# Expert products with a narrower gather ring, one resident half of the query weights, and weighted sums on four 64x64 quadrants

## The chip, the cores and the metric

The kernel runs on one core of a Trainium2 chip. The metric is the device time of one execution in microseconds. Three executions of the kernel before took 1419.11 us in the median (1418.01 to 1419.7); the execution that was profiled took 1418.62 us, of which the span from its first to its last instruction is 1416.6 us.

## The reference

Two transformer blocks follow each other on 256 tokens of width 1024, all in float32. The change lies in the second block, at its end. There the attention's result is added to `x`, and then each token is sent through experts:

```python
h2 = rms_norm(x, g_ffn) * (1.0 + scale2) + shift2
x = x + gate2 * peer_ffn(h2, w_peer_q, peer_keys1, peer_keys2, peer_u, peer_v)
return rms_norm(x, g_final)
```

```python
q = (hc @ w_q).reshape(-1, PEER_HEADS, PEER_KEY_DIM)         # 8 heads
...                                                          # top 16 of 128 x 128 keys for each head
g = softmax(best_s)
act = gelu(einsum('cd,chkd->chk', hc, u[expert]))            # one dot product for each expert
out = einsum('chk,chkd->cd', g * act, v[expert])             # weighted sum of rows of v
```

Each token has 8 x 16 = 128 experts of its own, and each expert is a row of 1024 numbers of `u` and one of `v`.

## The kernel before

The 256 tokens are two tiles of 128, one token on each partition. A *set* `n` (0 to 255) is one expert for each token of a tile: sets 0 to 127 belong to tile 0, 128 to 255 to tile 1. For each set five engines do one step, in this order:

- GpSimd (POOL, L2594) issues an indirect DMA, the *gather*: for each of 128 tokens one row of `peer_uv` (u and v side by side, 8 KB), 1 MiB in all, into a *ring slot*.
- VectorE (L2392) multiplies the u half with the tokens and sums: the *product*.
- ScalarE (L1544) takes the gelu of it.
- GpSimd (L2566) lays a 128x128 *diagonal* matrix with the weight of each token.
- TensorE (L1116) multiplies this diagonal with the v half, 1024 columns in two halves, and adds into two PSUM banks: the *sum*. With the sum the ring slot is free again.

The order on each engine is written out by hand. Each engine has a function `until(tick)` that does its step for all sets up to a tick, and between such calls stands the rest of tile 1's work (projections, attention, output rows, queries). TensorE's sums stand two ticks behind (`LAG`). GpSimd runs a loop over the gathers: before gather `n` into a slot that held set `b`, it lays the diagonals up to `b + LEAD` (`LEAD` is 2) and then waits for the sum of `b`. So with `m` slots gather `n` needs the diagonal of set `n - m + 2` and the sum of set `n - m`. The function `slot_table` deals the slots out in turn; `JOIN` says at which set further slots join.

Before, seven slots are there at first: `first_slot`, a tile of its own, and six halves of the weight ring `wr` (three tiles of 2 MiB), which are free when `w_out` and the query weights `w_peer_q` have been used for tile 0. `xc` joins at set 7, three places of the arena at set 88 and two more at set 118; so there are 8 slots to set 87, 11 to set 117, 13 then.

Tile 1's weights for the second block come once more from memory, in 18 *pieces* of 0.86 or 1 MiB which SyncE loads (L551, L560) into three buffers of the arena, later two, in turn; each waits for the piece that its buffer held. Pieces 0 and 1 are loaded before the ring starts, 2 to 4 just before, the rest beside the gathers. Pieces 14 to 17 are the query weights, used by `peer_queries` (L1087). The logits of the queries against the keys are `key_scores` (L1098), and the products of tile 1's output rows with `w_out` stand at L1277.

When all sums of a tile are there, VectorE multiplies them with the gate and adds them to `x` (L2490 and L2492 for tile 1, in two halves of 512 columns; the first half waits for `half_done`, the second for `pe_used`).

Of the kernel before, what the change touches and what calls it, by code (L numbers as in the profile page):

```python
# [26 lines left out]
SLOTS, DIAGS, LAG, LEAD = 7, 8, 2, 2  # L27
# [155 lines left out]
JOIN = {SLOTS: 1, 88: 3, 118: 2}  # L183
# [114 lines left out]
def program(nc, A, out):  # L298
    ctx = ExitStack()
    with ctx:  # L300
# [100 lines left out]
        piece = [region(kb0, KT * 256) for kb0 in (50, 58, 66)]  # L401
# [40 lines left out]
        p_in = [sem(f"p_in{i}") for i in range(3)]  # L442
# [44 lines left out]
        def _(sp):  # L487
# [18 lines left out]
            for i, (name, src, k, cols, _, _) in enumerate(blocks):  # L506
# [32 lines left out]
                if name == "tok":  # L539

                    sp.wait_ge(s["wuk_zero"], 1)
                    sp.dma_start(wuk[:, :, ROPE:], A["w_uk_2"][0]).then_inc(s["small_in"], 16)
# [4 lines left out]
                    for n, key in enumerate(("peer_keys1_2", "peer_keys2_2")):
                        sp.dma_start(keys[:, n * 64:(n + 1) * 64], A[key][0]).then_inc(s["ffg_in"], 16)
                    sp.wait_ge(s["ada_used"], 12)
                    for j in range(2):  # L550
                        sp.dma_start(piece_land(j), pieces[j]).then_inc(p_in[j], 16)  # L551
# [4 lines left out]
            for j in range(2, len(pieces)):  # L556
# [1131 lines left out]
        def _(dve):  # L1688
# [677 lines left out]
            def until(tick):  # L2366

                while dotted[0] < min(tick, SETS):
# [116 lines left out]
            dve.wait_ge(s["half_done"], 1)  # L2485
            for n in range(2):
                c = slice(n * BANK, (n + 1) * BANK)
                if n:
                    dve.wait_ge(s["pe_used"], SETS)
                chain(V.tensor_tensor(gated[:, n, :], bank[n][:, :], modb[:, 3, c], ALU.mult))  # L2490
                chain.wait()
                V.tensor_tensor(x[:, 1, c], x[:, 1, c], gated[:, n, :], ALU.add).then_inc(s["x_final"], 1)  # L2492
# [10 lines left out]
        def _(pool):  # L2503
# [66 lines left out]
            for n in range(SETS):  # L2570
# [5 lines left out]
                if n == 1:  # L2576
                    pool.wait_ge(s["wout_ready"], 2)
                elif n == 3:
                    pool.wait_ge(s["pair_ready"], filled("pq01"))
                elif n == 5:  # L2580
                    pool.wait_ge(s["pair_ready"], filled("pq03"))
                elif n == SLOTS:
                    pool.wait_ge(s["h2_done"], 1)
                elif n in JOIN:
                    if JOIN[n] == 3:
                        pool.wait_ge(s["pv_ready"], 2 * UNITS)
                        pool.wait_ge(s["oss_done"], 4)
                    else:
                        pool.wait_ge(s["pair_ready"], filled("ks13b"))
# [31 lines left out]
```

## Time and profile before

| | us |
|---|---|
| median of three executions | 1419.11 |
| profiled execution | 1418.62 |
| its span | 1416.6 |
| TensorE busy | 1297.8 (92%) |
| VectorE busy | 833.9 (59%) |
| GpSimd busy | 428.2 (30%) |
| gathers (software queue), share of the 16 DMA engines' span | 47.5%, 275.99 MB |
| SyncE's transfers (hardware queue) | 30.2%, 154.50 MB |

Times in the trace count from the first instruction. The gathers begin at 725.65 us and the last product is done at about 1406 us, so the expert stage is nearly half of the execution. A busy share is an average over the whole span; the stage has its own limits, which the rows below show. TensorE's busy time there contains the time in which a matmul's result is still on its way, so two matmuls overlap in it.

### The profile page before, as it was taken

The numbers are of one execution on the slowest core, as the hardware profiler recorded it, in microseconds if no ns is written. First come the engines' busy times: TensorE is split into PE (matmuls) and PEld (weight loads), VectorE is DVE, ScalarE is ACT, GpSimd is POOL, SyncE is SP. The second block draws the span as 40 slices with busy tenths as digits, with TensorE's granted clock in tenths as the row PEclk, the third lists the DMA queues.
The fourth block names the chain that finished last, engine by engine and source line by source line (L and its number), as shares of the span: only waits on it lengthen the run. The fifth ranks groups of instructions, "written<-read, shape, count | busy, mean of one in ns | idle before, by whom it ended". The sixth has DMA issues, their size and how long they took to land.

```text
span 1416.6 us, 15143 instructions
## 1 busy us (share of the span) xinstructions
PE 1297.8 (92%) x5447; PEld 837.6 (59%) x5447; DVE 833.9 (59%) x2027; ACT 275.0 (19%) x670; POOL 428.2 (30%) x554
## 2 busy tenths in 40 slices
PE   7999999999999999999989999989997777777776
PEld 6888888888687777757666644445642222222222
DVE  3553466213138888733486678757666767766654
ACT  2013100130010000033333234432220112111101
POOL 0101030000100000000024455555566555655551
PEclk9999999999999999999999999999999999999999
DMA  8345665224468888577369999999999999999995
GB/s 290 121 159 190 230 139 179 79 101 149 134 238 316 291 314 290 185 263 280 120 273 423 422 424 420 422 411 410 425 425 425 425 426 424 426 425 426 425 427 229
DMA packets 120202, 431.46 MB, mean 305 GB/s; under 512 B 10950, under 2 KB 34956, under 8 KB 84544
## 3 DMA queue, kind: packets, MB, share of 16 engines
q0 software_dynamic: 37904, 275.99, 47.5%
q1 hardware_dynamic: 82224, 154.50, 30.2%
q8 instruction: 44, 0.72, 0.2%
q14 instruction: 30, 0.25, 0.0%
HBM read 429.23 MB, written 1.24 MB: 304 GB/s over the span
## 4 chain that ended last, share of the span: by engine, by line
PE 59%; DMA 29%; DVE 3%; issue 3%; POOL 3%; ACT 2%; SPq 0%; POOLq 0%; DVEq 0%; ACTq 0%
PE psum L588 31%; DMA wr<-peer_uv,arena 13%; DMA arena<-peer_uv,arena 9%; PE psum L1116 6%; PE psum L890 4%; DMA first_slot<-peer_uv,arena 4%; DMA xc<-peer_uv,arena 3%; PE psum L968 2%; PE psum L866 2%; PE psum L941 2%; PE psum L1134 1%; POOL arena L2566 1%; PE psum L639 1%; POOL wr L2594 1%; PE psum L1178 1%
## 5 line engine op out<-in xcount | busy, mean ns | idle before, releaser
L588 PE MATMUL psum<-hT,wr 128*128 128x256 f32 x1792 | 391.6, 380 | 1.8 <-DMA wr<-in_w_in 1.8
L588 PEld LDWEIGHTS psum<-hT,wr 128*128 128x128 f32 x1792 | 339.1, 190 | 51.7 <-issue 6.0
L1116 PE MATMUL psum<-wr,arena 128*128 128x512 f32 x576 | 276.0, 609 | 39.1 <-POOL arena L2566 38.9
L2392 DVE CUSTOM_DVE_ANT_0 wr<-psum,wr 128x1024 f32<-128x1024 f32 x144 | 176.1, 1223 | 108.8 <-DMA wr<-peer_uv,arena 108.6
L1116 PEld LDWEIGHTS psum<-wr,arena 128*128 128x128 f32 x576 | 102.6, 193 | 178.9 <-issue 177.7
L2566 POOL TENSOR_SCALAR arena<-cst,arena 128x128 f32<-128x128 f32 x256 | 121.4, 474 | 171.5 <-ACT arena L1544 163.3
L2594 POOL DMA_INDIRECT wr<-peer_uv,arena x144 | 144.0, 1000 | 84.5 <-PE psum L1116 60.7
L1116 PE MATMUL psum<-arena 128*128 128x512 f32 x256 | 125.9, 616 | 33.6 <-POOL arena L2566 33.6
L1544 ACT ACTIVATE arena<-arena 128x1 f32<-128x1 f32 x256 | 50.9, 202 | 488.1 <-DVE arena L2392 487.8
L2392 DVE CUSTOM_DVE_ANT_0 arena<-psum,arena 128x1024 f32<-128x1024 f32 x64 | 78.4, 1224 | 55.5 <-DMA arena<-peer_uv,arena 55.5
L1116 PEld LDWEIGHTS psum<-arena 128*128 128x128 f32 x256 | 44.2, 191 | 111.4 <-issue 111.3
L2549 POOL TENSOR_TENSOR arena<-arena 128x512 f32<-128x512 f32 x11 | 16.9, 1538 | 217.6 <-DVE arena L1719 217.6
L2008 DVE SCALAR_TENSOR_TENSOR arena<-arena,csil 128x512 f32<-128x512 f32 x96 | 79.2, 825 | 3.0
L1717 DVE TENSOR_SCALAR arena<-psum,vec 128x256 f32<-128x256 f32 x68 | 29.8, 479 | 86.4 <-PE psum L588 78.5
L1719 DVE SCALAR_TENSOR_TENSOR arena<-psum,vec,arena 128x255 f32<-128x255 f32 (+1 forms) x160 | 69.7, 477 | 2.8
L2594 POOL DMA_INDIRECT arena<-peer_uv,arena x64 | 64.4, 1006 | 19.8 <-issue 11.3
L2594 POOL DMA_INDIRECT first_slot<-peer_uv,arena x24 | 24.0, 998 | 123.1 <-DVE arena L2340 108.4
L1116 PE MATMUL psum<-first_slot,arena 128*128 128x512 f32 x96 | 47.9, 622 | 8.6 <-POOL arena L2566 8.6
L588 PE MATMUL psum<-arena,wr 128*128 128x256 f32 x256 | 55.7, 379 | 0.0
L890 PE MATMUL psum<-wr,arena 128*128 128x512 f32 x128 | 55.6, 592 | 0.0
L1116 PE MATMUL psum<-xc,arena 128*128 128x512 f32 x96 | 46.3, 604 | 7.3 <-POOL arena L2566 7.1
L588 PEld LDWEIGHTS psum<-arena,wr 128*128 128x128 f32 x256 | 48.5, 190 | 7.3 <-issue 0.8
(350 smaller groups left out, 1422.6 us busy)
## 6 DMA issues: line engine op xcount, KB each, us to landing
wr<-in_w_in SPq DMA_DIRECT2D x22, 2048.0 KB, 8.8
arena<-in_w_ada SPq DMA_DIRECT2D x12, 2048.0 KB, 9.9
wr<-in_w_up SPq DMA_DIRECT2D x22, 1024.0 KB, 8.3
arena<-piece SPq DMA_DIRECT2D x16, 1024.0 KB, 9.1
wr<-in_w_down SPq DMA_DIRECT2D x5, 2048.0 KB, 9.7
wr<-in_w_a_out SPq DMA_DIRECT2D x2, 2048.0 KB, 8.1
wr<-in_w_b_out SPq DMA_DIRECT2D x2, 2048.0 KB, 8.6
wr<-in_w_o SPq DMA_DIRECT2D x2, 2048.0 KB, 8.1
```

What stands on the lines that cost most here:

```text
L588: mm = nc.tensor.matmul(bank[p % 4][:, f * S:(f + 1) * S], slot(i)[:, k, n * P:(n + 1) * P], act[:, k, :], start=k == 0, stop=k == KT - 1)
L866: mm = nc.tensor.matmul(bank[4 + 2 * n + t][:, :], sgb[:, k, t * P:(t + 1) * P], slot(23 + n)[:, k, :], start=k == 0, stop=k == KT - 1)
L890: mm = nc.tensor.matmul(bank[4 + 2 * n + t][:, :], act_ffn[:, f, t * P:(t + 1) * P], slot(i)[:, row, n * BANK:(n + 1) * BANK], start=f == ...
L941: mm = nc.tensor.matmul(o[:, 0:2 * cols], hT[:, k, tiles_of[t]], slot(at[name])[:, k, :], start=k == 0, stop=k == KT - 1)
L1116: mm = nc.tensor.matmul(bank[(6, 0)[t] + half][:, :], diag[:, n % DIAGS, :], gring[slot_of][:, D + half * BANK:D + (half + 1) * BANK], sta ...
L1544: A_(col, dots[:, t, c:c + 1], ACT.Gelu).then_inc(s["gelu_done"], 1)
L1717: ins = V.tensor_scalar(dst[:, n, :], src[:, n, :], w, None, ALU.mult)
L1719: ins = V.scalar_tensor_tensor(out=dst[:, n, back:S], in0=src[:, n, 0:S - back], scalar=w, in1=dst[:, n, back:S], op0=ALU.mult, op1=ALU.add)
L2008: ins = V.scalar_tensor_tensor(out=part, in0=ada[j % 2][:, k, :], scalar=csil[:, k:k + 1], in1=part, op0=ALU.mult, op1=ALU.add)
L2392: V.tensor_tensor_reduce(gring[slot_of][:, 0:D], h2[t], gring[slot_of][:, 0:D], 1.0, 0.0, ALU.mult, ALU.add, dots[:, t, c:c + 1]).then_inc ...
L2566: G.tensor_scalar(diag[:, n % DIAGS, :], ident, wgt[:, t, c:c + 1], gsoft[:, t, c:c + 1], ALU.mult, ALU.mult).then_inc(s["diag_done"], 1)
L2594: G.indirect_dma_start(gring[slot_of], None, A["peer_uv"], bass.IndirectOffsetOnAxis(ap=eid[:, t, c:c + 1], axis=0)).then_inc(g_in[slot_of ...
```

## The change

Four edits that belong together:

- `SLOTS` goes from 7 to 4: at first the ring has the four `wr` halves that are free when `w_out` and the first half of the query weights are used. `xc` joins at set 4, `first_slot` at set 18, the three arena places at 88 as before, and at 118 the two arena places together with the last two `wr` halves. So there are 5 slots to set 17, 6 to set 87, 9 to set 117 and 13 then.
- The second half of the query weights stays in `wr`; tile 1's queries 2 and 3 use it there, and pieces 16 and 17 are not loaded.
- Piece 5 gets a fourth buffer, `first_slot`, and is loaded with pieces 0 and 1 before the ring starts. Gather 18, the first into `first_slot`, waits until it has been used (`kb1b`).
- A sum is four matmuls on 64x64 quadrants instead of two on the whole array. The diagonal has two blocks that aren't zero, tokens 0 to 63 and tokens 64 to 127; each block multiplies each half of the columns. The results lie crosswise in the two banks, so `add_experts` needs four multiplications with the gate (64 partitions each) instead of two. The first of them waits for all sums; `half_done` is gone.

```diff
-SLOTS, DIAGS, LAG, LEAD = 7, 8, 2, 2
+SLOTS, DIAGS, LAG, LEAD = 4, 8, 2, 2
-JOIN = {SLOTS: 1, 88: 3, 118: 2}
+JOIN = {SLOTS: 1, 18: 1, 88: 3, 118: 4}
+PIECES = len(PIECE_FROM) - 2
-        b = j % 3 if j < PIECE_WIDE else j % 2
+        b = PIECE_BUFFER[j] if j < len(PIECE_BUFFER) else j % 2
-PIECE_WIDE = 10
+PIECE_BUFFER = (0, 1, 2, 0, 1, 3, 2, 0, 1, 2)
-        gring = [first_slot[:, :]] + gring
-        gring += [xc[:, 0:2 * D]] + [region(kb0, 2 * D) for kb0 in (8, 19, 70, 50, 58)]
+        gring = halves_of[:SLOTS] + [xc[:, 0:2 * D], first_slot[:, :]]
+        gring += [region(kb0, 2 * D) for kb0 in (8, 19, 70, 50, 58)] + halves_of[SLOTS:]
...
-                if t == 0:
+                if t == 0 or j >= 2:
                     weights(at["wpq"] + j // 2)
...
-                    for half in range(2):
-                        mm = nc.tensor.matmul(bank[(6, 0)[t] + half][:, :], diag[:, n % DIAGS, :],
-                                              gring[slot_of][:, D + half * BANK:D + (half + 1) * BANK], start=c == 0, stop=c == P - 1)
-                        if n == SETS - 1 and half == 0:
-                            mm.then_inc(s["half_done"], 1)
+                    for i, cols in ((0, 0), (1, 1), (0, 1), (1, 0)):
+                        own = quarters[i]
+                        mm = nc.tensor.matmul(bank[(6, 0)[t] + i][quarters[cols], :], diag[own, n % DIAGS, own],
+                                              gring[slot_of][own, D + cols * BANK:D + (cols + 1) * BANK], start=c == 0, stop=c == P - 1)
                     mm.then_inc(s["pe_used"], 1)
...
+            def add_experts(t, first):
+                for n in range(2):
+                    c = slice(n * BANK, (n + 1) * BANK)
+                    for i, own in enumerate(quarters):
+                        chain(V.tensor_tensor(gated[own, n, :], bank[first + i][quarters[n], :], modb[quarters[n], 3, c], ALU.mult))
+                    chain.wait()
+                    V.tensor_tensor(x[:, t, c], x[:, t, c], gated[:, n, :], ALU.add).then_inc(s["x_final"], 1)
```

GpSimd at the start of the ring, before: eight gathers (L2594) go out before the first three diagonals (L2566), and the ninth is the first that waits for a sum.

```order
L2594 DMA first_slot<-peer_uv,arena 128x2048 [waits eid_done]
L2594 DMA wr<-peer_uv,arena 128x2048 [waits wout_ready]
L2594 DMA wr<-peer_uv,arena 128x2048
L2594 DMA wr<-peer_uv,arena 128x2048 [waits pair_ready]
L2594 DMA wr<-peer_uv,arena 128x2048
L2594 DMA wr<-peer_uv,arena 128x2048 [waits pair_ready]
L2594 DMA wr<-peer_uv,arena 128x2048
L2594 DMA xc<-peer_uv,arena 128x2048 [waits h2_done]
L2566 TENSOR_SCALAR arena<-cst,arena 128x128 [waits gelu_done,norm_done]
L2566 TENSOR_SCALAR arena<-cst,arena 128x128 [waits gelu_done] x2
L2594 DMA first_slot<-peer_uv,arena 128x2048 [waits pe_used]
```

The same place now (the gather stands at L2597, the diagonal at L2570):

```order
L2597 DMA wr<-peer_uv,arena 128x2048 [waits eid_done,wout_ready]
L2597 DMA wr<-peer_uv,arena 128x2048
L2597 DMA wr<-peer_uv,arena 128x2048 [waits pair_ready]
L2597 DMA wr<-peer_uv,arena 128x2048
L2597 DMA xc<-peer_uv,arena 128x2048 [waits h2_done]
L2570 TENSOR_SCALAR arena<-cst,arena 128x128 [waits gelu_done,norm_done]
L2570 TENSOR_SCALAR arena<-cst,arena 128x128 [waits gelu_done] x2
L2597 DMA wr<-peer_uv,arena 128x2048 [waits pe_used]
```

Three gathers fewer stand ahead of the first diagonals, and the sixth gather is now the first that waits for a sum.

SyncE's pieces at the end of its list, before: pieces 5 to 17 (L560) and the last transfers of its list.

```order
L551 DMA arena<-piece 128x1760 [waits ada_used]
L551 DMA arena<-piece 128x1760
L522 DMA wr<-in_w_in 128x8x512 [waits down_ready] x2
...
L560 DMA arena<-piece 128x2048 [waits pair_ready] x5
L560 DMA arena<-piece 128x2048 [waits piece_used]
L560 DMA arena<-piece 128x2048 [waits pair_ready] x2
...
L560 DMA arena<-piece 128x2048 [waits wout_ready]
L560 DMA arena<-piece 128x2048 [waits pair_ready] x2
L562 DMA arena<-in_g_final 128x1024 [waits eid_done]
```

The same places now (L552 and L561):

```order
L552 DMA arena<-piece 128x1760 [waits ada_used]
L552 DMA arena<-piece 128x1760
L552 DMA first_slot<-piece 128x2048
L523 DMA wr<-in_w_in 128x8x512 [waits down_ready] x2
...
L561 DMA arena<-piece 128x2048 [waits pair_ready] x4
L561 DMA arena<-piece 128x2048 [waits piece_used]
L561 DMA arena<-piece 128x2048 [waits pair_ready]
...
L561 DMA arena<-piece 128x2048 [waits wout_ready]
L563 DMA arena<-in_g_final 128x1024 [waits eid_done]
```

One piece has moved up in front of the weights of tile 0's projections, and the last two, which waited for `pair_ready`, are gone.

TensorE at the first sums, before: two matmuls of 512 columns for a sum (L1116), with tile 1's projections (L968) between.

```order
L1116 MATMUL psum<-first_slot,arena 128x512 [waits diag_done,g_in0]
L1116 MATMUL psum<-first_slot,arena 128x512
L985 MATMUL psum<-cst,arena 128x128 [waits bank_free1,lat_done]
L985 MATMUL psum<-cst,arena 128x128 x3
L1116 MATMUL psum<-wr,arena 128x512 [waits diag_done,g_in1]
```

And now (L1118):

```order
L1118 MATMUL psum<-wr,arena 64x512 [waits diag_done,g_in0]
L1118 MATMUL psum<-wr,arena 64x512 x3
L986 MATMUL psum<-cst,arena 128x128 [waits bank_free1,lat_done]
L986 MATMUL psum<-cst,arena 128x128 x3
L1118 MATMUL psum<-wr,arena 64x512 [waits diag_done,g_in1]
```

The order of sums and other work is the same; only the matmuls of a sum have changed.

## Rows read from the trace of the kernel before

**Rows 1.** The page: what the DMA engines moved, in 40 slices.

```profile
GB/s 290 121 159 190 230 139 179 79 101 149 134 238 316 291 314 290 185 263 280 120 273 423 422 424 420 422 411 410 425 425 425 425 426 424 426 425 426 425 427 229
```

**Rows 2.** Stretches: length, busy PE PEld DVE ACT POOL, PEclk, DMA share, GB/s.

```profile
740.00:940.00 200.00, 193.59 (x671) 105.18 (x670) 146.93 (x420) 70.67 (x166) 107.07 (x145) 0.97 1.01 422
940.00:960.00 20.00, 15.19 (x54) 9.84 (x53) 11.16 (x27) 5.52 (x14) 8.33 (x12) 0.83 0.97 390
...
1050.00:1400.00 350.00, 272.09 (x562) 95.20 (x560) 231.21 (x580) 54.55 (x169) 199.53 (x274) 1.00 1.01 424
```

**Rows 3.** The page's DMA issues: count, KB each, median us to landing.

```profile
arena<-piece SPq DMA_DIRECT2D x16, 1024.0 KB, 9.1
```

**Rows 4.** SyncE's timeline: issue of piece 5, and of piece 17.

```profile
750.71 0.33 SPq L560 DMA_DIRECT2D arena<-piece  x1
...
1014.22 0.33 SPq L560 DMA_DIRECT2D arena<-piece  x1
```

**Rows 5.** The gathers (L2594): from issue to landing.

```profile
DMA to landing us min/median/max: 5.7/24.0/26.9
```

**Rows 6.** GpSimd's timeline: gather 0, the first diagonals, gather 8.

```profile
725.65 1.03 POOL L2594 DMA_INDIRECT first_slot<-peer_uv,arena  x1 [108.36 <-DVE arena L2340]
...
738.22 1.73 POOL L2566 TENSOR_SCALAR arena<-cst,arena 128x128 f32<-128x128 f32 x3
742.84 1.00 POOL L2594 DMA_INDIRECT first_slot<-peer_uv,arena  x1 [2.89 <-PE psum L1116]
```

**Rows 7.** VectorE's timeline: products of sets 5, 8 and 76.

```profile
744.86 1.22 DVE L2392 CUSTOM_DVE_ANT_0 wr<-psum,wr 128x1024 f32<-128x1024 f32 x1 [0.73 <-DMA wr<-peer_uv,arena]
...
752.34 1.22 DVE L2392 CUSTOM_DVE_ANT_0 first_slot<-psum,first_slot 128x1024 f32<-128x1024 f32 x1 [0.34 <-DMA first_slot<-peer_uv,arena]
...
940.90 1.23 DVE L2392 CUSTOM_DVE_ANT_0 wr<-psum,wr 128x1024 f32<-128x1024 f32 x1 [0.90 <-DMA wr<-peer_uv,arena]
```

**Rows 8.** TensorE's timeline: sums 0, 8, 9; a step of attention; sums 76, 77.

```profile
738.81 3.75 PE L1116 MATMUL psum<-first_slot,arena 128*128 128x512 f32 x4 [3.14 <-POOL arena L2566]
...
765.72 1.88 PE L1116 MATMUL psum<-first_slot,arena 128*128 128x512 f32 x4
767.44 1.88 PE L1116 MATMUL psum<-wr,arena 128*128 128x512 f32 x4
...
851.52 0.70 PE L1036 MATMUL psum<-arena 64*128 64x256 f32 x2
...
864.13 0.70 PE L1036 MATMUL psum<-arena 64*128 64x256 f32 x2
...
947.94 3.78 PE L1277 MATMUL psum<-arena,hT 128*128 128x256 f32 x8 [4.81 <-ACT hT L1439]
951.51 3.85 PE L1116 MATMUL psum<-wr,arena 128*128 128x512 f32 x8
```

**Rows 9.** TensorE's timeline: matmuls on parts of the array (rows*columns of it).

```profile
129.00 1.06 PE L686 MATMUL psum<-arena,cst 128*32 128x512 f32 x8
...
246.64 2.08 PE L749 MATMUL psum<-arena 64*64 64x64 f32 x64
...
279.97 2.08 PE L767 MATMUL psum<-arena 64*64 64x64 f32 x32
```

**Rows 10.** ScalarE's timeline: gelu of sets 5 and 6.

```profile
750.62 0.29 ACT L1544 ACTIVATE arena<-arena 128x1 f32<-128x1 f32 x2
```

**Rows 11.** The end: last product, diagonal and sum; VectorE's first gate and add.

```profile
1405.13 1.23 DVE L2392 CUSTOM_DVE_ANT_0 arena<-psum,arena 128x1024 f32<-128x1024 f32 x1 [1.19 <-DMA arena<-peer_uv,arena]
...
1406.77 0.45 POOL L2566 TENSOR_SCALAR arena<-cst,arena 128x128 f32<-128x128 f32 x1 [1.98 <-ACT arena L1544]
...
1407.36 1.96 PE L1116 MATMUL psum<-arena 128*128 128x512 f32 x4 [0.47 <-POOL arena L2566]
...
1408.50 0.69 DVE L2490 TENSOR_TENSOR arena<-psum,arena 128x512 f32<-128x512 f32 x1 [2.13 <-PE psum L1116]
1409.22 0.69 DVE L2492 TENSOR_TENSOR x<-x,arena 128x512 f32<-128x512 f32 x1
```

More of the change, by code:

```diff
@@ L266, in piece_rows @@
     out = []
-    for w, c, n in PIECE_FROM:
+    for w, c, n in PIECE_FROM[:PIECES]:
         block = inputs[w][0][:, c:c + n].reshape(KT, P, n)
@@ L283, in piece_places @@
 def piece_places():
-    out, turns, before = [], [0, 0, 0], [None, None, None]
-    for j in range(len(PIECE_FROM)):
-        b = j % 3 if j < PIECE_WIDE else j % 2
+    out, turns, before = [], [0] * 4, [None] * 4
+    for j in range(PIECES):
+        b = PIECE_BUFFER[j] if j < len(PIECE_BUFFER) else j % 2
         out.append((b, turns[b], before[b]))
@@ L400, in program @@
         score, work, negA = region(30, S), region(31, S), region(32, S)
-        piece = [region(kb0, KT * 256) for kb0 in (50, 58, 66)]
+        piece = [region(kb0, KT * 256) for kb0 in (50, 58, 66)] + [first_slot[:, :]]
         lgs = [region(66, 4 * 2 * P).rearrange("p (r u s) -> p r u s", r=4, u=2),
@@ L441, in program @@
         g_in = [sem(f"g_in{i}") for i in range(SLOTS + sum(JOIN.values()))]
-        p_in = [sem(f"p_in{i}") for i in range(3)]
+        p_in = [sem(f"p_in{i}") for i in range(4)]
         bank_free = [sem(f"bank_free{i}") for i in range(4)]
@@ L451, in program @@
         ab = wr[6 % NS][:, 0:KT * (32 + H)].rearrange("p (k n) -> p k n", k=KT)
-        pieces = [A[f"piece{j}"] for j in range(len(PIECE_FROM))]
+        pieces = [A[f"piece{j}"] for j in range(PIECES)]
         wpq0 = next(i for i, b in enumerate(blocks) if b[0] == "wpq")
-        gring = [wr[(wpq0 + i // 2 - 1) % NS][:, (i % 2) * 2 * D:(i % 2 + 1) * 2 * D] for i in range(SLOTS - 1)]
-        gring = [first_slot[:, :]] + gring
-        gring += [xc[:, 0:2 * D]] + [region(kb0, 2 * D) for kb0 in (8, 19, 70, 50, 58)]
+        halves_of = [wr[(wpq0 + i // 2 - 1) % NS][:, (i % 2) * 2 * D:(i % 2 + 1) * 2 * D] for i in range(2 * NS)]
+        gring = halves_of[:SLOTS] + [xc[:, 0:2 * D], first_slot[:, :]]
+        gring += [region(kb0, 2 * D) for kb0 in (8, 19, 70, 50, 58)] + halves_of[SLOTS:]
         def piece_at(j):
@@ L549, in _ @@
                     sp.wait_ge(s["ada_used"], 12)
-                    for j in range(2):
-                        sp.dma_start(piece_land(j), pieces[j]).then_inc(p_in[j], 16)
+                    for j in (0, 1, 5):
+                        sp.dma_start(piece_land(j), pieces[j]).then_inc(p_in[PIECE_PLACE[j][0]], 16)
                 if name == "wo" and blocks[i - 1][0] == "wo":
@@ L554, in _ @@
                     sp.dma_start(nfg, A["norm_final_g"].partition_broadcast(P)).then_inc(s["row_in"], 16)
-            for j in range(2, len(pieces)):
+            for j in (2, 3, 4, *range(6, PIECES)):
                 b, _, before = PIECE_PLACE[j]
@@ L2484, in _ @@
             until(SETS)
[L2485 to L2492, printed above, removed]
+            dve.wait_ge(s["pe_used"], SETS)
+            add_experts(1, 0)
             dve.wait_ge(s["x_final"], 4)
@@ L2575, in _ @@
                     laid += 1
-                if n == 1:
+                if n == 0:
                     pool.wait_ge(s["wout_ready"], 2)
-                elif n == 3:
+                elif n == 2:
                     pool.wait_ge(s["pair_ready"], filled("pq01"))
-                elif n == 5:
-                    pool.wait_ge(s["pair_ready"], filled("pq03"))
                 elif n == SLOTS:
                     pool.wait_ge(s["h2_done"], 1)
[L2584 to L2589, printed above, removed]
+                elif n == 18:
+                    pool.wait_ge(s["pair_ready"], filled("kb1b"))
+                elif n == 88:
+                    pool.wait_ge(s["pv_ready"], 2 * UNITS)
+                    pool.wait_ge(s["oss_done"], 4)
+                elif n == 118:
+                    pool.wait_ge(s["pair_ready"], filled("ks13b"))
                 if n % PK == 0:
```

5 lines of the change are left out of this document (3 added, 2 removed).

## The prediction, as it went on record

> **What bounds the kernel now.** I read the page's row of GB/s first. The reader is to see that from the twenty-second slice on, with slices of 35.4 us from about 744 us, the 16 DMA engines move 410 to 427 GB/s until the end, and that no slice before the ring is over 316 [rows 1]. The stretches say the same: DMA share 1.01 at 422 GB/s in 740 to 940 us and at 424 in 1050 to 1400, while VectorE and GpSimd have gaps; the only dent is 940 to 960 us, with 390 GB/s at a granted clock of 0.83 [rows 2]. TensorE shows 194 busy of 200 us there, but products of VectorE wait for a DMA ("0.34 <-DMA", "0.90 <-DMA") [rows 7]. So the expert stage ends when its bytes are moved, and 1 MiB costs 1.0486 MB / 424 GB/s = 2.47 us. What counts is (a) how many bytes lie in the saturated stretch, (b) whether the queue ever runs dry, (c) what is added before the ring or behind its last byte. Next I read GpSimd's and TensorE's timelines at the start of the ring and at the output rows, to see who returns slots when, and the tail last.
>
> A gather that meets an empty queue takes 5.7 us from issue to landing, the least of all; the median of 24.0 is mostly queueing [rows 5]. With m slots, gather n needs the diagonal of set n-m+2 and the sum of set n-m. In the undisturbed tail a product starts at 1405.13, its diagonal is done at 1407.22, its sum starts at 1407.36 [rows 11]. From product to diagonal are 2.09 us, from product to the end of a sum of 1.06 us 3.3 us.
>
> **Bytes.** Pieces 16 and 17 are gone, and piece 5 is loaded before the ring. All three are 1 MiB [rows 3] and lay in the saturated stretch: piece 5 was issued at 750.71, piece 17 at 1014.22 [rows 4]. 3 x 2.47 = 7.4 us less. The early load of piece 5 goes beside work with at least a quarter of the bandwidth free [rows 1], so I cost it at 0; without that cover it would be its 2.47.
>
> **The sum on quadrants.** Four matmuls of 2 records instead of two, so 8 records. One sum of 4 records takes 1.72 us from start to start and 1.88 by itself [rows 8]. The trace shows no sum on four quadrants, but four column strips do 8 records of 512 columns in 1.06 us, and 64 small matmuls on a pair of quadrants take the same 2.08 us as 32 on one [rows 9]. Bounds: 1.06 us if all four run beside each other, about 3.5 (8 records at 0.43) if they take turns; I take 1.06, the row with the same columns. The saving of 0.66 us a sum is itself worth nothing while DMA is the bound. It only makes slots return sooner.
>
> The Trainium skill ("TensorEngine Tiling (Array Packing)", section Key Properties) says that tiles operate independently, but also that a change of the tiling mode drains TensorE; it speaks against this change, since sums alternate with full-array work. The 1.06 us stood in a stream of full-array work, so the trace bears out the first half and shows no large price of the second [rows 9]. By the drain rule the time would be that of the slow rival below.
>
> **Start of the ring: +2.0.** Before, eight gathers went out before the first diagonal (which ran at 738.22), and gather 8 was issued at 742.84, right behind sum 0, which took 3.75 us from 738.81 [rows 6, 8]; the queue never dried. Now gather 5 waits for sum 0. If that sum takes about half of 3.75, so 2.0, gather 5 goes out at 738.81 + 2.0 + 0.3 = 741.1 and lands at 746.8. Product 5 began at 744.86 [rows 7]: about 2.0 late. Bounds: a sum of 1.06 makes it 1.0, one that is as slow as now 3.7.
>
> The Trainium skill ("DMA: Bandwidth & Descriptors", section "Anatomy of one DMA — SWDGE (gpsimd) path") gives a DMA of this kind about 2.0 us plus bytes over 436 GB/s, an estimated 4.4 us for 1 MiB; by it gather 5 would land at 745.5, the term would be 0.7 and the time 1415.7. The trace's least is 5.7 [rows 5], so I stay with the row.
>
> **Five slots, gathers 5 to 17: +0.7.** Landing of n follows product n-3 by 2.09 + 0.1 + 5.7 = 7.9 us, and three sets of transfers last 7.4. That leaves 0.16 a gather, 2.1 for 13. Besides, the gelu of set 5 runs only at 750.62, with that of set 6 [rows 10], 5.8 us after its product began; gather 8 needs that diagonal, goes out at about 751.5 and lands at 757.2, where product 8, two us later than its 752.34 [rows 7], would want 754.3: up to 2.9 more. Against holes of 5.0 stand pieces 6 to 8, 7.4 us of transfers which are wanted anyway and whose buffers come free in this stretch. I take 0.7, near the lower bound of 0; the upper one is 2.7 (the pieces fill less than half).
>
> **Six slots at the output rows: +1.3.** Product 76 runs at 940.90, but sum 76 stands behind a product of output rows which starts at 947.94 after 4.81 us of waiting for ScalarE and lasts 3.78; sum 76 begins at 951.51 [rows 7, 8]. With eight slots nobody needed it yet. Now gather 82 needs it: 951.5 + 1.06 + 0.3 = 952.9, landing at 958.6. Six sets of transfers after 940.90 are 955.7, so 2.9 late. The kernel before loses something here itself: 20 us at 390 instead of 424 GB/s are 1.6 us [rows 2], which the new hole contains. 2.9 - 1.6 = 1.3; bounds 0 (a piece stands in the queue) and 2.9. Elsewhere six slots allow a set 6 x 2.47 - 5.7 - 0.3 = 8.8 us from product to the end of its sum, which 3.3 and the queueing on a relieved TensorE fit into.
>
> **Tail: +1.3.** The gate waited for half a sum and began at 1408.50; four quadrants end at 1407.36 + 1.06 = 1408.4, so it begins as before. Then come six operations instead of four, the two new ones on 64 partitions and 512 columns. The old take 0.69 each, and follow each other after 0.72 [rows 11]. I take 0.65 each, by their columns; by their partitions the four would cost what two did, so the bounds are 0 and 1.4. The same two operations at set 164 lie beside 13 slots of slack: 0. If that cover is gone, they are 1.3 there too.
>
> **Sum.** -7.4 + 2.0 + 0.7 + 1.3 + 1.3 = -2.1 against the profiled execution's 1418.62 (span 1416.6): 1416.5. That execution was 0.5 under the median 1419.11, so the forecast is 1417.0 in terms of the median, 0.15% less. About 0.2%, 2.8 us, is what a measurement of this kernel can tell from no change; the forecast lies just within. With the terms' bounds its own range is 1412 to 1422.
>
> **Rivals.**
> *Faster by more than 0.2%.* The queue hardly dries: pieces fill the holes of the start, and the faster sums take away the dent at 940 us instead of deepening it. For it: pieces 6 to 15 are ten MiB or nearly, some 24 us of transfers that can lie in a hole wherever their buffer is free, and TensorE is relieved by 0.66 a sum. Against it: two places where the order itself holds a gather. Then -7.4 + 1.3 (tail), with 0.6 of the start left, is -5.5; without the start and the tail's cost -7.0: 1412.1 to 1413.6.
>
> *Slower.* The quadrants take turns, or every change between sums and full-array work costs TensorE, so that it can't return five or six slots in time. The place to tell is a step of attention: 851.52 to 864.13 is 12.6 us with five sums, 8.6 of them the sums at 1.72 and 4.0 the rest [rows 8]; five gathers are 12.35. TensorE becomes the bound there from (12.35 - 4.0) / 5 = 1.67 us a sum on. Even at today's 1.72, few slots don't do: from product 8 at 752.34 to the end of sum 8 at 767.4 are 15 us [rows 7, 8], and five slots allow 5 x 2.47 - 5.7 - 0.3 = 6.4. That is about 8.7 once at the start, and, with sums queued behind the output rows at some 15 against 8.8, about 6 there: -7.4 + 1.3 + 8.7 + 6 = +8.6, so 1424 to 1428, and more if a sum takes longer than 1.72. Against it: the 1.06 us [rows 9].
>
> *The bytes don't count.* The removed pieces merely leave idle bandwidth, because after 1014 us something else keeps the pace. Then the two pieces' 4.9 are not gained, and -7.4 + 4.9 + 5.3 (the four terms that cost) = +2.8, 1421.9. Against it: a share of 1.01 in 1050 to 1400 [rows 2].
>
> **Chances.** The sum as worked out (1412 to 1422, mostly 1414 to 1420) 0.50, the faster rival 0.30, the slow quadrants 0.14, bytes that don't count 0.06. Of the first, 0.09 lies under 1416.3, 0.38 within the 0.2% and 0.03 over it; of the faster rival 0.28 and 0.02; the slow quadrants count as slower, and the last case, at the limit, as the same. Faster: 0.09 + 0.28 = 0.37; same: 0.38 + 0.02 + 0.06 = 0.46; slower: 0.03 + 0.14 = 0.17. The range 1412 to 1422 leaves out the slow quadrants and the best end of the faster rival.
>
> **What will show it.** Bytes: SyncE's transfers fall by 2 MiB, and the last product comes about 7.4 us, less the holes, earlier. Quadrants: eight records of a sum in about 1.1 us in 1050 to 1400. Start: an idle gap of DMA between the landing of gather 4 and of 5, and product 5 at about 747. Five slots: gather 8 at about 751.5, GpSimd waiting for gelu. Output rows: a lower DMA share in 940 to 970 than the 0.97 now, gather 82 waiting for sum 76. Tail: six VectorE operations of about 0.65 us, the first at the end of the sum. I am wrong if a sum takes 1.7 us or more, if DMA's share is well below 1 in steps of attention, or if the ring loses nothing in its first 40 us.

## The result: 1.9% slower, and the profile after

The changed kernel takes 1448.22 us (median of four, 1442.68 to 1449.08) against 1419.4 us: a ratio of 1.0193, interval 1.0177 to 1.0209. The forecast was 1417.0 us, the range 1412 to 1422. The profiled execution has a span of 1446.2 us, 29.6 more than before.

The page of the changed kernel, its rows of granted TensorE clock and of GB/s in 40 slices (36.2 us each now), against [rows 1]:

```profile
PEclk9999999999999999999998978669887667666576
...
GB/s 284 118 157 191 235 124 171 118 59 172 150 211 326 334 295 301 124 371 178 186 282 339 414 349 375 338 394 378 426 426 425 426 425 424 426 425 425 425 426 228
```

Before, the DMA engines ran at 410 to 427 GB/s from the twenty-second slice to the last but one. Now six slices in that part lie lower, down to 338. The stretches of the changed kernel, with the columns of [rows 2]:

```profile
740.00:940.00 200.00, 151.65 (x848) 68.75 (x849) 130.85 (x373) 61.27 (x146) 93.45 (x127) 0.81 0.94 360
740.00:800.00 60.00, 48.44 (x310) 27.00 (x311) 33.08 (x89) 12.83 (x34) 26.31 (x35) 0.83 0.90 339
800.00:840.00 40.00, 28.25 (x151) 14.15 (x150) 26.14 (x79) 7.36 (x20) 18.29 (x25) 0.90 1.00 412
840.00:940.00 100.00, 74.96 (x390) 27.60 (x389) 71.63 (x207) 41.08 (x92) 48.84 (x67) 0.76 0.93 351
940.00:1000.00 60.00, 46.05 (x244) 20.45 (x242) 35.57 (x100) 15.88 (x40) 31.69 (x44) 0.76 0.96 377
1050.00:1400.00 350.00, 233.80 (x1208) 50.98 (x1206) 238.52 (x609) 56.19 (x175) 210.19 (x285) 0.70 1.01 425
```

Measured against 424 GB/s, transfer time is lost as 60 x (1 - 339/424) = 12.0 us in 740 to 800, 1.1 in 800 to 840, 17.2 in 840 to 940 and 6.7 in 940 to 1000: 37 us. The kernel before lost about 3: 1 in 740 to 940, at 422 GB/s [rows 2], and 2 in 940 to 1000, at 409:

```profile
940.00:1000.00 60.00, 52.48 (x175) 31.44 (x174) 39.90 (x102) 16.47 (x38) 32.45 (x42) 0.91 1.00 409
```

Once 9 and 13 slots are there the rate is 425 as before, with TensorE's granted clock at 0.70. The sum agrees: 34 us lost, 2.5 of a later first gather (728.15 against 725.65), 2.0 at the end, less 7.4 for three MiB, is 31 against the 29.6 measured. About 2 of the 2.5 are there at 20 us of the program: the first matmuls took longer, 28 instead of 37 had begun by then, at a granted clock of 1.00 in both. Nothing that the change touches had run. The profiled executions of e1, e4 and e5 below have it too (first gather at 727.78 to 728.65), those of e2, e3 and e8 not (725.96 to 726.35), so it goes with the execution and not with the change; its cause is not shown.

What a gather waits for has changed. GpSimd's waits in 740 to 1000 us, first of the kernel before (waiter, releaser, total us, times, longest):

```profile
POOL wr L2594 <- PE psum L1116: 48.0, 33, 4.8
POOL arena L2566 <- ACT arena L1544: 36.4, 26, 5.0
```

and of the changed kernel:

```profile
POOL arena L2570 <- ACT arena L1544: 92.3, 54, 5.0
POOL wr L2597 <- PE psum L1118: 20.9, 12, 4.4
```

Before, GpSimd sat mostly on sums, to no harm: enough gathers stood in the queue, and the rate stayed at 422 GB/s [rows 2]. Now it sits on the gelu of the diagonal that has to be laid ahead of a gather, and the queue is shorter. From issue to landing the gathers of 740 to 940 us took, before and now:

```profile
DMA to landing us min/median/max: 8.2/11.7/16.1
DMA to landing us min/median/max: 5.5/8.4/13.1
```

Three places show how. The start of the ring on GpSimd (the fifth gather, then the sixth, the first that needs a sum):

```profile
733.25 0.93 POOL L2597 DMA_INDIRECT xc<-peer_uv,arena  x1 [0.30 <-issue]
...
742.47 0.66 POOL L2570 TENSOR_SCALAR arena<-cst,arena 128x128 f32<-128x128 f32 x1 [0.47 <-ACT arena L1544]
743.99 1.00 POOL L2597 DMA_INDIRECT wr<-peer_uv,arena  x1 [0.86 <-PE psum L1118]
...
754.32 0.45 POOL L2570 TENSOR_SCALAR arena<-cst,arena 128x128 f32<-128x128 f32 x1 [3.37 <-ACT arena L1544]
754.93 1.00 POOL L2597 DMA_INDIRECT wr<-peer_uv,arena  x1 [0.16 <-issue]
```

Gather 5 goes out at 743.99, gather 8 at 754.93, right behind the diagonal of set 5. VectorE's products 5 and 8, against [rows 7]:

```profile
749.55 1.22 DVE L2402 CUSTOM_DVE_ANT_0 wr<-psum,wr 128x1024 f32<-128x1024 f32 x1 [2.01 <-DMA wr<-peer_uv,arena]
...
761.74 1.22 DVE L2402 CUSTOM_DVE_ANT_0 wr<-psum,wr 128x1024 f32<-128x1024 f32 x1 [3.64 <-DMA wr<-peer_uv,arena]
```

Product 5 is 4.7 later than before, of which 2.5 are the later start; product 8 is already 9.4 later. The second place is in attention, with six slots. VectorE, ScalarE and GpSimd around set 62:

```profile
931.29 1.22 DVE L2402 CUSTOM_DVE_ANT_0 xc<-psum,xc 128x1024 f32<-128x1024 f32 x1
```

```profile
930.44 1.28 ACT L1498 ACT_TABLE_LOAD   x1
...
933.45 1.28 ACT L1518 ACT_TABLE_LOAD   x1
...
935.06 1.28 ACT L1544 ACT_TABLE_LOAD   x1
```

```profile
930.75 1.00 POOL L2597 DMA_INDIRECT wr<-peer_uv,arena  x1 [0.20 <-issue]
936.73 0.45 POOL L2570 TENSOR_SCALAR arena<-cst,arena 128x128 f32<-128x128 f32 x1 [4.98 <-ACT arena L1544]
937.38 1.11 POOL L2597 DMA_INDIRECT first_slot<-peer_uv,arena  x1 [0.20 <-issue]
```

Product 62 is done at 932.5, but ScalarE is in exponentials, a sum of squares and a root, with three table loads of 1.28 us, and comes to gelu 62 at 936.36. The diagonal starts at 936.73, and gather 66, whose slot's sum had been done since 930.8, goes out 6.6 us after gather 65. The kernel before has the same ScalarE work; there, with eight slots, the gather that waits for diagonal 62 is number 68, two sets further on.

The third place is the output rows, as forecast. GpSimd waits for sum 76 before gather 82, and the rate falls:

```profile
983.10 0.99 POOL L2597 DMA_INDIRECT wr<-peer_uv,arena  x1 [4.17 <-PE psum L1118]
```

```profile
980.00:990.00 10.00, 10.00 (x57) 5.21 (x56) 5.73 (x12) 0.41 (x2) 4.45 (x6) 0.90 0.75 277
```

The sum itself came out as forecast. TensorE, two sums of eight records at either clock:

```profile
828.18 1.09 PE L1118 MATMUL psum<-xc,arena 64*64 64x512 f32 x8
...
962.66 1.99 PE L1118 MATMUL psum<-first_slot,arena 64*64 64x512 f32 x8 [1.10 <-POOL arena L2570]
```

The granted clock is 1.00 in 827 to 830 us and 0.50 in 962 to 965. So at 2.4 GHz all four quadrants together take 1.09 us, at 1.2 GHz 1.99. The end, VectorE's last product and the gate:

```profile
1432.69 1.23 DVE L2402 CUSTOM_DVE_ANT_0 wr<-psum,wr 128x1024 f32<-128x1024 f32 x1 [1.24 <-DMA wr<-peer_uv,arena]
...
1436.58 1.40 DVE L2248 TENSOR_TENSOR arena<-psum,arena 64x512 f32<-64x512 f32 x2 [2.65 <-PE psum L1118]
1438.01 0.69 DVE L2250 TENSOR_TENSOR x<-x,arena 128x512 f32<-128x512 f32 x1
1438.74 1.42 DVE L2248 TENSOR_TENSOR arena<-psum,arena 64x512 f32<-64x512 f32 x2
```

A multiplication on 64 partitions costs 0.70 us, as much as one on 128 [rows 11].

### The profile page after: what moved, and what is told of

It is laid out like the page before. It is cut to its first block, busy times and chain, and to the rows that moved or that the text cites. A ratio compares the mean times of both kernels' runs of the same rounds, so it can differ in the third digit from the quotient of the medians.

```text
span 1446.2 us, 17194 instructions
## 1 busy us (share of the span) xinstructions
PE 1219.1 (84%) x6471; PEld 739.5 (51%) x6471; DVE 836.7 (58%) x2031; ACT 274.5 (19%) x670; POOL 428.0 (30%) x554
## 4 chain that ended last, share of the span: by engine, by line
PE 51%; DMA 35%; DVE 5%; issue 3%; ACT 3%; POOL 2%; SPq 0%; POOLq 0%; DVEq 0%; ACTq 0%
PE psum L589 31%; DMA wr<-peer_uv,arena 14%; DMA arena<-peer_uv,arena 11%; DMA first_slot<-peer_uv,arena 6%; DMA xc<-peer_uv,arena 4%; PE psum L891 4%; PE psum L867 2%; PE psum L1118 2%; PE psum L942 1%; PE psum L1134 1%; POOL arena L2570 1%; DVE wr L2402 1%; PE psum L969 1%; PE psum L640 1%; PE psum L1178 1%
## 5 line engine op out<-in xcount | busy, mean ns | idle before, releaser
L1118 PE MATMUL psum<-wr,arena 64*64 64x512 f32 x1104 | 207.8, 836 | 86.5 <-POOL arena L2570 86.4
L2402 DVE CUSTOM_DVE_ANT_0 wr<-psum,wr 128x1024 f32<-128x1024 f32 x138 | 168.8, 1223 | 131.5 <-DMA wr<-peer_uv,arena 131.1
L2570 POOL TENSOR_SCALAR arena<-cst,arena 128x128 f32<-128x128 f32 x256 | 121.8, 476 | 247.7 <-ACT arena L1544 226.4
L2597 POOL DMA_INDIRECT wr<-peer_uv,arena x138 | 138.1, 1001 | 159.6 <-DVE arena L2349 108.7
L1118 PEld LDWEIGHTS psum<-wr,arena 64*64 64x64 f32 x1104 | 38.8, 166 | 216.1 <-issue 214.3
L1118 PE MATMUL psum<-arena 64*64 64x512 f32 x512 | 93.8, 817 | 54.5 <-POOL arena L2570 54.5
L1118 PEld LDWEIGHTS psum<-arena 64*64 64x64 f32 x512 | 18.0, 160 | 127.0 <-issue 126.6
L2597 POOL DMA_INDIRECT arena<-peer_uv,arena x64 | 63.7, 995 | 14.0 <-issue 12.6
L1118 PE MATMUL psum<-xc,arena 64*64 64x512 f32 x224 | 42.5, 838 | 21.5 <-POOL arena L2570 21.3
L1118 PE MATMUL psum<-first_slot,arena 64*64 64x512 f32 x208 | 39.2, 831 | 20.1 <-POOL arena L2570 20.1
L891 PE MATMUL psum<-wr,arena 128*128 128x512 f32 x128 | 55.6, 592 | 0.0
L2402 DVE CUSTOM_DVE_ANT_0 xc<-psum,xc 128x1024 f32<-128x1024 f32 x28 | 34.2, 1222 | 23.1 <-DMA xc<-peer_uv,arena 22.9
```

The costliest lines, as they stand in the source:

```text
L891: mm = nc.tensor.matmul(bank[4 + 2 * n + t][:, :], act_ffn[:, f, t * P:(t + 1) * P], slot(i)[:, row, n * BANK:(n + 1) * BANK], start=f == ...
L1118: mm = nc.tensor.matmul(bank[(6, 0)[t] + i][quarters[cols], :], diag[own, n % DIAGS, own], gring[slot_of][own, D + cols * BANK:D + (cols + ...
L2402: V.tensor_tensor_reduce(gring[slot_of][:, 0:D], h2[t], gring[slot_of][:, 0:D], 1.0, 0.0, ALU.mult, ALU.add, dots[:, t, c:c + 1]).then_inc ...
L2570: G.tensor_scalar(diag[:, n % DIAGS, :], ident, wgt[:, t, c:c + 1], gsoft[:, t, c:c + 1], ALU.mult, ALU.mult).then_inc(s["diag_done"], 1)
L2597: G.indirect_dma_start(gring[slot_of], None, A["peer_uv"], bass.IndirectOffsetOnAxis(ap=eid[:, t, c:c + 1], axis=0)).then_inc(g_in[slot_of ...
```

## The experiments

Theory A: with five and six slots, a gather is issued so late, and mostly behind a diagonal, that the queue runs short; each delay anywhere shows in the transfer rate. Theory B: the quadrants leave TensorE idle, its clock falls, and its other work is late. Each run is compared with runs of the kernel before on the same chip (1418.9 to 1419.7 us).

**Sums on the whole array, all else changed (e1).**

```diff
-for i, cols in ((0, 0), (1, 1), (0, 1), (1, 0)): ... diag[own, n % DIAGS, own] ...
+for half in range(2): ... diag[:, n % DIAGS, :] ...
```

> The changed kernel, but each sum again two matmuls on the whole array (and the gate again two multiplications of 128 partitions, behind the last sum). Theory A (few slots: each gather waits for a diagonal two sets on, and every delay empties the queue) expects no gain: 1440 to 1460 us, because a sum of 1.72 us returns slots even later, and a DMA rate in 740 to 1000 us that stays under 390 GB/s. Theory B (the quadrants leave TensorE idle, its granted clock falls to 0.7 to 0.8 in 840 to 960 us, and everything TensorE does there is late) expects the clock back near 0.96 and the time back at 1412 to 1425 us.

1447.44 us, ratio 1.020 (1.0168 to 1.0232). Its stretches 740 to 940 and 1050 to 1400 us:

```profile
740.00:940.00 200.00, 179.62 (x600) 95.19 (x601) 131.16 (x374) 61.87 (x149) 95.45 (x130) 0.94 0.94 367
...
1050.00:1400.00 350.00, 281.49 (x646) 106.90 (x645) 237.39 (x606) 56.27 (x175) 210.74 (x285) 0.99 1.01 425
```

The clock is back, the time is not: theory B's 1412 to 1425 us did not come.

**Quadrants alone, in the kernel before (e2).** The diff's sum and `add_experts`, nothing else.

> The kernel before, with its 8, 11 and 13 slots and all 18 pieces, but each sum on four quadrants and the gate in four multiplications. Theory A expects 1419 + 1.3 for the gate = 1419 to 1422 us: with 8 slots the queue doesn't dry whatever the clock does. Theory B expects the granted clock at 0.7 to 0.9 from 740 us on, as in the changed kernel, and a time over 1428 us.

1420.59 us, ratio 1.0008 (0.9996 to 1.0021). Its same stretches:

```profile
740.00:940.00 200.00, 165.48 (x966) 73.59 (x962) 145.22 (x418) 70.29 (x165) 106.89 (x147) 0.85 1.01 418
...
1050.00:1400.00 350.00, 231.01 (x1128) 41.88 (x1128) 232.88 (x582) 54.44 (x169) 200.48 (x274) 0.69 1.01 424
```

With nearly the same low clock as in the changed kernel, but the slots of the kernel before, the time is that of the kernel before. With e1, theory B falls: neither the quadrants nor the clock is the loss.

**One diagonal less ahead of a gather, in the changed kernel (e3).**

```diff
-SLOTS, DIAGS, LAG, LEAD = 4, 8, 2, 2
+SLOTS, DIAGS, LAG, LEAD = 4, 8, 2, 1
```

> The changed kernel, with LEAD 1 for 2: gather n needs the diagonal of set n-m+1 instead of n-m+2, so it may go out one set (2.47 us) earlier wherever the diagonal is what it waits for. Theory A expects that most of the 34 us of lost transfer in 740 to 1000 us goes: 1418 to 1432 us. Theory B expects the sums to stay late and no change or little: 1440 to 1450 us.

1432.24 us, ratio 1.0093 (1.0069 to 1.0117): 16 us back. Its stretches 740 to 940 and 740 to 800, and GpSimd's two largest waits in 740 to 1000 us:

```profile
740.00:940.00 200.00, 161.99 (x934) 73.11 (x935) 139.19 (x400) 69.25 (x161) 102.59 (x141) 0.85 0.97 391
740.00:800.00 60.00, 55.34 (x365) 31.86 (x363) 37.40 (x100) 16.23 (x40) 30.44 (x41) 0.89 0.98 400
```

```profile
POOL arena L2570 <- ACT arena L1544: 50.2, 40, 5.0
POOL wr L2597 <- PE psum L1118: 48.3, 28, 6.9
```

About half of the 34 us was the wait for the diagonal two sets on, where theory A expected most of it. The start has most of its loss back: 400 GB/s in 740 to 800 us instead of 339. The two waits are now even: the sum is late next.

**Pieces 16 and 17 loaded again (e4).**

```diff
-PIECES = len(PIECE_FROM) - 2
+PIECES = len(PIECE_FROM)
-if t == 0 or j >= 2:
+if t == 0:
```

> The changed kernel, with pieces 16 and 17 loaded and used again (slots, quadrants and the early piece 5 as in the changed kernel). If the 2 MiB count where the engines are saturated, the time is 4.9 us longer, 1453 us; if they only filled idle bandwidth, it stays at 1448 us. The two theories on the loss say the same here.

1450.72 us (1444.71 to 1451.83), 2.5 over the changed kernel. With such spread it lies between both answers and decides nothing alone.

**Six slots alone, in the kernel before (e5); the same with LEAD 1 (e6); seven slots with LEAD 1 (e7).** No byte removed, whole-array sums.

```diff
-SLOTS, DIAGS, LAG, LEAD = 7, 8, 2, 2
+SLOTS, DIAGS, LAG, LEAD = 5, 8, 2, 2
-JOIN = {SLOTS: 1, 88: 3, 118: 2}
+JOIN = {SLOTS: 1, 88: 3, 118: 4}
```

(e6: LEAD 1; e7: SLOTS 6, three places at 118, LEAD 1.)

> The kernel before with six slots from the start to set 87 (9 to 117, 13 then) in place of eight: two weight halves stay out of the ring until set 118. All 18 pieces, whole-array sums, LEAD 2, no byte less. Theory A (slots) expects most of the changed kernel's lost transfer here too, without any other part of the change: 34 us less what the sixth slot saves at the start, so 1438 to 1452 us. Theory B (the sums' form and clock) and a theory C (the way the pieces were re-ordered) expect 1419 to 1423 us.

> As the run with six slots, but LEAD 1. Theory A with the diagonal as the releaser expects about half of the loss back, as in the changed kernel with LEAD 1 (16 us): 1425 to 1436 us. If the sum is the releaser here (whole-array sums are later), there is little change from six slots.

> The kernel before with seven slots to set 87 (10 to 117, 13 then) and LEAD 1, else unchanged. Theory A: seven sets of transfers are 17.3 us, less 5.7 and 0.3 leaves 11.3 us from a product to the end of its sum; the sums at attention steps reach about 11, so the ring just holds: 1419 to 1425 us. A theory by which every slot costs the same expects half of the loss of six slots.

1443.34 us (1.0163; 1.0146 to 1.018), 1433.56 (1.0097; 1.008 to 1.0114) and 1424.63 (1.0027; 1.0012 to 1.0042). This is the main cause by itself: two slots less, with nothing else touched, cost 24 us. LEAD 1 gives 10 of them back, a seventh slot 9 more. In 740 to 940 us the DMA engines moved 378 GB/s with six slots, 392 with LEAD 1, 412 with seven:

```profile
740.00:940.00 200.00, 182.87 (x610) 98.29 (x611) 133.47 (x382) 63.12 (x150) 96.23 (x131) 0.93 0.96 378
```

```profile
740.00:940.00 200.00, 190.04 (x640) 101.07 (x639) 137.61 (x394) 69.12 (x160) 101.39 (x137) 0.95 0.97 392
```

```profile
740.00:940.00 200.00, 193.22 (x658) 103.33 (x658) 144.68 (x416) 70.13 (x165) 106.48 (x143) 0.96 1.00 412
```

**The changed kernel with piece 5 back beside the gathers, six slots from the start (e8).**

```diff
-for j in (0, 1, 5):
+for j in (0, 1):
-gring = halves_of[:SLOTS] + [xc[:, 0:2 * D], first_slot[:, :]]
+gring = [first_slot[:, :]] + halves_of[:SLOTS - 1] + [xc[:, 0:2 * D]]
```

> The changed kernel with piece 5 loaded beside the gathers again and first_slot in the ring from gather 0, so six slots from the start (quadrants, kept query weights and LEAD 2 as changed). The start (740 to 800 us) lost 12 us of transfer with five slots; the theory that each slot of the ring counts expects about 8 of these back for 2.5 us of piece: 1441 to 1445 us. If the start's loss comes from TensorE's other work there, it is 1449 to 1452 us.

1437.34 us, ratio 1.0128 (1.0111 to 1.0145): 10.9 less than the changed kernel with one more MiB in the saturated stretch, and below both answers. 1443.3 for six slots, less 4.9 for pieces 16 and 17, is 1438.4, near this run's 1437.3. That fits the price of the bytes but does not show it, since this run also has the quadrants and the longer end, and its rate in 740 to 940 us is 385 GB/s where six slots alone had 378. If piece 5 is worth its 2.5, five slots at the start cost 10.9 + 2.5 = 13.4 us.

**Six slots, quadrants and LEAD 1 (e9), and the order of the other engines (e10, e13, e17).** On e9: TensorE's sums one tick earlier (e10), ScalarE's gelus one tick later (e13) and one tick earlier (e17).

```diff
-SLOTS, DIAGS, LAG, LEAD = 5, 8, 2, 1        (e9)
+SLOTS, DIAGS, LAG, LEAD = 5, 8, 1, 1        (e10)
-while laid[0] < min(tick - 1, SETS):        (e9)
+while laid[0] < min(tick - 2, SETS):        (e13; e17: tick)
```

> The changed kernel with piece 5 back beside the gathers (six slots from the start) and LEAD 1. If the two repairs add, 1437.3 less the 10 that LEAD 1 gave with six slots: 1425 to 1430 us. If the start's loss and LEAD's are the same transfers, 1432 to 1437 us.

> As the run before it (six slots, quadrants, LEAD 1), and TensorE's sums one tick earlier in its order (LAG 1 for 2; VectorE's order as it was). If what is left is sums that stand behind a waiting attention or output matmul, they return slots about 2.5 us earlier: 1416 to 1424 us. If an earlier sum makes TensorE wait for its diagonal and so delays attention, which sets the pace of the products, there is no change or a loss: 1426 to 1434 us.

> The changed kernel with six slots from the start and LEAD 1 (1429.6 us), and ScalarE's gelus one tick later in its order, so that its copies and exponentials stand one set earlier. What is lost there still lies in 840 to 1000 us (385 and 378 GB/s). If it comes from sums that stand behind an attention matmul which waits for a ScalarE copy that stands behind a gelu of a set three ahead, the chain is one set (2.47 us) shorter: 1420 to 1426 us. If the later gelu, and so the later diagonal, costs as much as that gives, 1428 to 1436 us.

> The changed kernel with six slots and LEAD 1 (1429.6 us), and ScalarE's gelus one tick earlier in its order, the mirror of the run with them one tick later (1439.4). If the time follows the diagonal, 1420 to 1427 us; if ScalarE's copies and exponentials are held up by the earlier gelus and hold the sums, 1432 to 1442 us.

In this order: 1429.64 us (1.0074; 1.0049 to 1.0099), 1434.61 (1.0117; 1.0087 to 1.0147; from 1427.73 to 1439.97), 1439.39 (1.0131; 1.011 to 1.0152) and 1431.91 (1.0089; 1.0072 to 1.0107). The two repairs add, but no order tried gets the rest: a later gelu costs 10 us, more than either answer had, an earlier one and earlier sums gain nothing. So my theory that ScalarE's copies behind later gelus hold the sums is not borne out. e9 would be about 1416 if it lost nothing (1419.4 - 4.9 + 1.3 for the gate); which waits make up its remaining 14 us is open. Its largest waits in 840 to 1000 us are for sums:

```profile
POOL wr L2595 <- PE psum L1118: 41.8, 21, 6.5
POOL arena L2570 <- ACT arena L1544: 21.6, 15, 2.9
```

**A short ring to the end, in the kernel before: six slots (e15), five (e16).** As e5, with `JOIN = {SLOTS: 1}`; after 1050 us only sums and routing are left. One execution each.

> The kernel before with six slots to the end (whole-array sums, LEAD 2): after 1050 us nothing but sums and routing is left, so the ring is seen alone. Gather n goes out 2.1 + 0.2 us after product n-4 and needs 5.6 to land, 7.9 in all, against 4 x 2.47 = 9.9. If a gather in flight moves at full rate whatever stands behind it, 1050 to 1400 us stay at 424 GB/s. If the engines move less while few gathers are queued (372 GB/s per unit of busy share at 880 to 920 us in the changed kernel, 418 in the kernel before), the stretch is at 380 to 415 GB/s with a share near 1.

> As the run with six slots to the end, but five. Gather n now follows product n-3: 7.9 us against 7.4. With full rate in flight that is a set each 2.63 us, 398 GB/s in 1050 to 1400 us; if few queued gathers are slower as well, 340 to 385 GB/s.

1454.96 and 1549.3 us. Three stretches of six slots, then of five:

```profile
1100.00:1200.00 100.00, 78.17 (x160) 27.14 (x160) 68.34 (x177) 13.68 (x46) 59.13 (x81) 1.00 1.01 420
1200.00:1300.00 100.00, 73.65 (x152) 25.86 (x152) 68.99 (x184) 19.95 (x52) 56.90 (x76) 1.00 1.00 406
1300.00:1400.00 100.00, 77.08 (x156) 27.31 (x156) 61.07 (x145) 13.47 (x45) 56.74 (x78) 0.98 1.00 404
```

```profile
1100.00:1200.00 100.00, 74.01 (x174) 30.20 (x174) 55.41 (x147) 12.87 (x41) 48.02 (x65) 0.94 0.92 339
1200.00:1300.00 100.00, 68.56 (x139) 23.93 (x137) 61.05 (x158) 16.36 (x45) 50.30 (x69) 0.98 0.95 362
1300.00:1400.00 100.00, 69.52 (x140) 24.51 (x140) 61.66 (x164) 12.87 (x42) 52.89 (x71) 0.98 0.99 374
```

Even without attention, six slots move 404 to 420 GB/s at a share of 1.00 to 1.01, five 339 to 374 at 0.92 to 0.99, under the 398 that a full rate in flight would give. From issue to landing a gather took 7.6 us there in the median with six slots and 5.9 with five, against 24.8 in the kernel before: by estimate some three and two on their way, where ten were.

**Keeping eight slots (e11, e12, e14).** e11: piece 5 early with seven slots to set 23 and eight to 87, LEAD 1, quadrants for tile 0 only; e14 the same with whole-array sums; e12 only quadrants for tile 0.

```diff
-JOIN = {SLOTS: 1, 88: 3, 118: 2}
+JOIN = {SLOTS: 1, 24: 1, 88: 3, 118: 2}     (e11, e14; SLOTS 6, LEAD 1)
+if t == 0: ... four quadrants ...           (e11, e12)
```

> The kernel before with eight slots, but piece 5 before the ring (first_slot joins at set 24, seven slots until then), LEAD 1, and quadrants for tile 0's sums alone, so that the end is as before. The theory that bytes count and only short rings lose expects -2.5 for the piece and about -1.5 for the dent at 940 to 960 us, +0 to 1 at the start: 1415.0 to 1417.5 us. If seven slots at the start lose more than the piece, 1419 to 1422 us.

> The kernel before with quadrants for tile 0's sums alone (whole-array sums and the half-sum gate for tile 1). Against the kernel before only the dent at 940 to 960 us can go: 1417 to 1419.7 us; quadrants for all sums were 1420.6, of which 1.3 was put down to the gate at the end, so 1419.3 or less is expected.

> The kernel before with piece 5 loaded before the ring (first_slot joins at set 24, seven slots until then, eight to 87) and LEAD 1; all sums on the whole array. The run with quadrants for tile 0 was 1417.0 us. If the piece's 2.47 us are what was gained, this is 1416.5 to 1418 us too; if the quadrants were, it is 1419 to 1421 us.

1417.0 us (0.999; 0.9979 to 1.0001), 1420.06 (1.0002; 0.9993 to 1.0011) and 1418.95 (1.0003; 0.9994 to 1.0012). With eight slots nearly nothing is left of the loss, and the best version can't be told from the kernel before. e12 lies just over its range, and e14 between its two answers: the piece's 2.5 us did not show. No run is clearly faster than the kernel before.

## Why the prediction was wrong

- **What bounds the kernel** held: with 9 and 13 slots the rate is 425 GB/s, and the three things that count (bytes, a dry queue, ends) were the right ones. The second was far too small.
- **Bytes, -7.4**: not contradicted. e8 against e5 is -6.0, of which -4.9 would be pieces 16 and 17; e4 is unclear, e14 did not show piece 5's 2.5.
- **Start, +2.0**: right for gather 5. Sum 0 took 1.98 us. Product 5 came 4.7 late with 2.5 from the later first gather.
- **Five slots, +0.7, upper bound 2.7: the first step that failed.** Start and five slots cost 13.4 together by e8. The mechanism was named (gather n behind the diagonal of n-3, gelu of set 5 late, gather 8 late), but I let pieces 6 to 8 fill its holes. They didn't: 740 to 800 us ran at 339 GB/s. The pieces went out at 751.65, 758.51 and 774.47, and none in the deepest holes, 744 to 748 us at 188 GB/s and 784 to 788 at 197: a piece waits for its own buffer, not for the hole. And a product that comes late makes the next diagonal late too (product 5 is 4.7 late, product 8 9.4), so delays add up instead of being filled. With one diagonal less ahead (e3) the stretch ran at 400.
- **Six slots, "fit into": the step that cost most.** I compared 8.8 us with the time to the end of a sum, and left the diagonal out, which I had used one paragraph before. With LEAD 2 and six slots, gather n follows product n-4 by 7.9 us of 9.9: 2.0 us to spare, and no term for the attention steps, where ScalarE holds a gelu for 3 to 5 us. The stretch 840 to 940 lost 17 us. The DMA share of 0.93 there is one of the signs of being wrong that I had named. e5 shows the two missing slots alone (24 us), e6 what the diagonal two sets on has of it (10).
- **Output rows, +1.3**: the place and the wait were right. Gather 82 went out 30 us later than I had it, at 983.10, and the hole at 980 to 990 us lost 3.5 where 2.9 was forecast; 940 to 1000 as a whole lost 6.7 where the kernel before lost 2, the rest in steps for which I had no term.
- **Tail, +1.3**: 2.0 (from the last product to the span's end 13.5 us against 11.5). The gate's size was right (0.70 each); it began 3.89 us after the last product's start instead of 3.37 [rows 11], since the sum before it took 1.59 us instead of 1.06, at a granted clock of 0.67 in 1434 to 1437 us.
- **The rivals.** The slow one gave 1424 to 1428, on its wrong mechanism (a sum that takes 1.7 us or more); the sum took 1.09. Its second half, that few slots don't do at today's 1.72, is what e5 measured; its price was put at 8.7 + 6, and six slots alone cost 24. The drain after a change of tiling mode, which the Trainium skill states in "TensorEngine Tiling (Array Packing)", section Key Properties, has no visible price in the time of e2 (1.0008), where transfers are the bound. On TensorE the trace agrees with it: 16 full-array matmuls hold a quadrant sum back 1.98 us from their start (749.57 to 751.55), a whole-array sum 1.78 in the kernel before (748.73 to 750.51), and full-array work starts 1.02 us behind the start of a quadrant sum, a second quadrant sum 0.91. So a sum between full-array work saves TensorE 0.50 us, (1.78 + 1.72) - (1.98 + 1.02), and not my 0.66. The faster rival's -7.0 should be -7.4 by its own terms, which changes nothing here.

## What to carry to other kernels

In a ring of buffers the number to work out is how many transfers are in flight when the last condition of an issue is met, over all its conditions, not the slot count and not the wait that is largest in the profile: GpSimd's waits for sums, the largest before, were harmless while gathers enough stood behind them. A slot whose cover looks idle is the reserve from which every delay of every engine is paid; two slots of eight cost 24 us, five times the 4.9 us at which the two MiB that they were given up for were estimated. Where work laid ahead of a wait (LEAD) is itself late, laying one less ahead is worth a trial: it gave 16 us in e3 and 10 in e6.

## What was not expected of the hardware

- A busy DMA engine moved less in the kernels with few gathers queued. Per unit of busy share the changed kernel moved 360 / 0.94 = 383 GB/s in 740 to 940 us, the kernel before 422 / 1.01 = 418 [rows 2]; e16 368 to 381. So about half of the changed kernel's loss there is idle engines and half slower busy ones. What makes a busy engine slower was not tried.
- The granted clock fell to 0.70 in 1050 to 1400 us (a mean of the two levels), from 1.00, when TensorE had less to do (233.80 busy us of 350 against 272.09 [rows 2]), and at 1.2 GHz a sum takes 1.99 us, more than the 1.88 of the whole-array sum at 2.4 GHz that it replaced [rows 8]. There the change of form, with the fall of the clock, buys nothing.
